# Prompt attention's units at other steps of a page-streaming attention, with first queries and row constants rounded in other steps

## The reference, cut to what matters

```python
logit[t, s] = q_t . k_s / sqrt(Dh) + cq[t] - ck[s]       # 16 heads of 64; c: running sum of log forget
s = where(k_pos <= q_pos, s, -1e30)
p = softmax(s, axis=-1)
o = einsum('bhqk,bkhd->bqhd', p, v)
```

## Time and profile before

| | us |
|---|---|
| median of three runs | 1809.26 |
| lowest, highest | 1804.97, 1809.34 |
| profiled execution | 1808.28 |
| its span, first to last instruction | 1806.5 |
| TensorE busy, share of the span | 1741.4, 96% |
| VectorE, ScalarE, GpSimd busy | 1151.8, 885.1, 348.6 |
| the attention stage | about 972 to 1347 |

### The profile page before, as it was taken

How to read it: one execution, slowest core, us unless ns; L and a number is a source line. 1 busy time by engine, 2 the same in 40 slices (tenths; PEclk the granted TensorE clock), 3 DMA queues, 4 the chain that set the end, 5 groups by cost and what they waited for, 6 DMA issues and landing times. The chain is left out here.

```text
span 1806.5 us, 41781 instructions
## 1 busy us (share of the span) xinstructions
PE 1741.4 (96%) x16593; PEld 1616.2 (89%) x16593; DVE 1151.8 (64%) x2113; ACT 885.1 (49%) x1579; POOL 348.6 (19%) x261
## 2 busy tenths in 40 slices
PE   8999999999999999999998999999989999999998
PEld 7999998889999999999997677776769999999998
DVE  4766775579828828555653466666656994595481
ACT  5355445465525524455632455555555653354252
POOL 3333332000120130333531011112200004003012
PEclk9999999899999999999999999999999999999999
DMA  5333222323423332342356999999983334234232
GB/s 129 85 108 85 83 84 66 87 79 94 118 71 94 95 94 71 87 147 62 117 172 205 384 374 379 385 385 367 366 287 99 94 94 117 61 97 115 57 100 70
DMA packets 291541, 273.79 MB, mean 152 GB/s; under 512 B 22034, under 2 KB 252531, under 8 KB 290836
## 3 DMA queue, kind: packets, MB, share of 16 engines
q1 hardware_dynamic: 289412, 268.63, 45.8%
q10 hardware_dynamic: 1792, 1.44, 0.3%
q0 software_dynamic: 144, 1.05, 0.2%
HBM read 254.64 MB, written 16.43 MB: 150 GB/s over the span
## 5 line engine op out<-in xcount | busy, mean ns | idle before, releaser
L2117 PE MATMUL ps<-xh,f_l 128*128 128x288 f32 x1232 | 279.2, 298 | 0.2 <-DVE f_l L2373 0.2
L2137 PE MATMUL ps<-f_h,f_l 128*128 128x288 f32 x1748 | 243.0, 296 | 0.2 <-DVE t_small L2482 0.2
L2137 PEld LDWEIGHTS ps<-f_h,f_l 128*128 128x128 f32 x1748 | 236.1, 189 | 0.4 <-DVE t_small L2482 0.4
L2117 PEld LDWEIGHTS ps<-xh,f_l 128*128 128x128 f32 x1232 | 208.6, 189 | 0.6 <-DVE f_l L2373 0.5
L2117 PE MATMUL ps<-xl,f_l 128*128 128x288 f32 x704 | 208.3, 296 | 0.0
L2117 PE MATMUL ps<-f_l 128*128 128x288 f32 x1056 | 156.8, 297 | 7.6 <-ACT t_small L2264 4.2
L2447 DVE TENSOR_TENSOR xT<-xT,ps 128x576 f32<-128x576 f32 x48 | 36.2, 754 | 197.1 <-PE ps L2137 197.1
L1586 DVE COPY at_kt<-ps 128x512 f32<-128x512 f32 x128 | 88.2, 691 | 109.7 <-PE ps L1289 109.2
L2117 PEld LDWEIGHTS ps<-f_l 128*128 128x128 f32 x1056 | 146.2, 189 | 9.0 <-ACT t_small L2264 5.0
L2117 PEld LDWEIGHTS ps<-xl,f_l 128*128 128x128 f32 x704 | 133.6, 190 | 0.0
L653 POOL TENSOR_TENSOR a_wl<-a_wraw,a_wh 128x1024 fp32r<-128x1024 f32 x32 | 78.5, 2456 | 200.6 <-ACT a_wh L548 185.4
(11 more groups left out here) (434 smaller groups left out, 4064.4 us busy)
## 6 DMA issues: line engine op xcount, KB each, us to landing
xT<-in_cache_k SPq DMA_DIRECT2D x40, 512.0 KB, 6.1
xT<-in_cache_v SPq DMA_DIRECT2D x40, 512.0 KB, 6.6
a_wraw<-in_a_w_in SPq DMA_DIRECT2D x32, 512.0 KB, 4.2
f_h_plain<-in_cache_k SPq DMA_DIRECT2D x30, 512.0 KB, 6.4
xl_plain<-in_cache_v SPq DMA_DIRECT2D x30, 512.0 KB, 6.5
f_h_plain<-in_cache_v SPq DMA_DIRECT2D x30, 512.0 KB, 7.0
xl_plain<-in_cache_k SPq DMA_DIRECT2D x29, 512.0 KB, 6.3
a_wraw<-in_w_gate_up SPq DMA_DIRECT2D x44, 256.0 KB, 4.1
```

What stands on the lines that cost most here:

```text
L2117: mm = pe.matmul(place(m, pos), wt[:, at], combination(2 * q, part, b), start=pos in (0, 1, 3) and t == 0 and i == 0, stop=t == len(pairs) ...
L2137: mm = pe.matmul(ps[:, first + a, 0:HALF], wt[:, at], hidden(i, part)[:, a * HALF:(a + 1) * HALF], start=opens and t == 0 and y == 0, stop ...
```

## The change

The head pairs' first steps are spread evenly from step 9 to step 64: 9, 16, 24, 32, 40, 48, 56, 64 in place of 15, 22, 29, 36, 43, 50, 57, 64. Within a head pair nothing changes: four steps, and the turns one step later. `unit_rows` and the casts of later queries move with the starts. The first head pair's query casts (`query_high(0)`) move from step 9 to step 4, and the rounding of the row constants from step 2 to step 4, where it stands before those casts.

```diff
-    FIRST_UNIT, PAIR_STEPS, PARTS_AT, OUT_AT, TAIL_AT = 15, 7, 4, 5, 6
+    PARTS_AT, OUT_AT, TAIL_AT = 4, 5, 6
+    FIRST_UNIT, LAST_UNIT = 9, KSTEPS
+    STARTS = [FIRST_UNIT + j * (LAST_UNIT - FIRST_UNIT) // (KD - 1) for j in range(KD)]
...
+    def unit_at(n):
+
+        j = sum(start <= n for start in STARTS) - 1
+        return j, n - STARTS[max(j, 0)]
+
     def unit_pair(n):
 
-        j, i = divmod(n - FIRST_UNIT, PAIR_STEPS)
-        return 4 * j + i if 0 <= j < KD and i < 4 else None
+        j, i = unit_at(n)
+        return 4 * j + i if j >= 0 and i < 4 else None
...
-                j = (n - AHEAD - 3 - FIRST_UNIT) // PAIR_STEPS + 1
-                if (n - AHEAD - 3 - FIRST_UNIT) % PAIR_STEPS == 0 and 1 <= j < KD:
-                    unit_rows(j)
+                if n - AHEAD - 3 in STARTS[:-1]:
+                    unit_rows(STARTS.index(n - AHEAD - 3) + 1)
...
-                if n == 2:
+                if n == 4:
                     act.wait_ge(e["headed"], 16)
                     act.activation(rowl[:], headrow, ACT.Copy).then_inc(e["fixed"], 1)
...
-                j, i = divmod(n - FIRST_UNIT, PAIR_STEPS)
-                if i == OUT_AT and 0 <= j < KD:
+                j, i = unit_at(n)
+                if i == OUT_AT and j >= 0:
                     output(j)
-                if n == FIRST_UNIT - 6:
+                if n == 4:
                     query_high(0)
                 if i == PARTS_AT and 0 <= j < KD - 1:
                     query_high(j + 1)
```

## The result

The changed kernel takes 1812.44 us in the median of 18 runs (1808.81 to 1816.20), the kernel before 1808.57 us (18 runs, 1802.99 to 1811.02): a ratio of 1.0025, 95% interval 1.0017 to 1.0034, so 3.1 to 6.1 us slower.

A forecast was written before the change was run, and what follows sets the result against it. TensorE was taken as the bound. Terms of 7.7 (units), -3.4, -1.7, +0.9 and +0.5 summed to +4.0 us on 1808.28, so 1812.3, stated as 1812.5; 8 in 10 range 1802 to 1819.

The forecast's parts named there:

- TensorE bound, parts add: Attention steps: TensorE is the bound, a step costs its parts' prices, and each microsecond it waits lengthens the span.
- Six groups at 8c: Head pairs starting at 16, 24 to 56, with a sequence's first exponential: 2.45 us of stalls each, 14.7 in all.
- First group: Head pair at steps 9 to 13: stalls like those of steps 57 to 61, 1.8 us.
- Part 2: Row constants rounded at step 4 instead of 2: ScalarE's wait for their transfer goes, gaining 3.4 us.
- Part 3: First queries cast at step 4 instead of 9: 1.7 us gained at step 10, 0.9 lost at step 5.
- The +0.9 for step 5: First query casts at step 4 make step 5's key copies late: 0.9 us lost (0 to 1.3).
- step 10 near its parts plus 0.8: Sign: step 10 would take about 0.8 us above its parts, though with a unit in it.
- Part 4: End of the stage, after light steps 61 to 63: last steps could wait for a page, +0.5 us (0 to 2).
- The sum: Whole kernel: all terms together +4.0 us, 1812.3 on the profiled execution, stated as 1812.5.
- The rival of the smoothed load: Units at a fixed place stall 3.5 us in place of 8.8: 1798.8 us; chance 0.15 for faster by over 0.3%.

The follow-up runs named there:

- E8: Changed kernel with the last key tile's four transposes done twice in the light steps from 21 on: 1821.58 us, ratio 1.0072 to the kernel before.
- E1: Kernel before with only the row constants rounded at step 4 instead of 2: 1805.97 us, ratio 0.9989.
- E5: Changed kernel with head pairs starting at 9, 17, 25, 33, 41, 49, 57, 64: 1811.14 us, ratio 1.0016 to the kernel before.
- E6: Changed kernel with head pairs starting at 10, 18, 26, 34, 42, 50, 57, 64: 1799.98 us, ratio 0.9959 to the kernel before.
- E7: Changed kernel with the sequence's exponential before the two unit exponentials in ScalarE's order within a step: 1804.13 us, ratio 0.9978 to the kernel before.
- E2: Kernel before with only the first queries cast at step 4 instead of 9: 1806.72 us, ratio 0.9993.
- E4: Changed kernel with the row constants back at step 2 and the first queries cast at step 3: 1814.75 us, ratio 1.0038 to the kernel before.
- E10: Kernel before with row constants and first query casts at step 4, and ScalarE's sequence exponential before the unit exponentials: 1801.33 us, ratio 0.9963.

## Why the prediction was right, step by step

- **TensorE bound, parts add.** Right, and shown by E8. Between kernels steps of the same make-up mostly agree within 0.03 us (a few within 0.1: step 31 took 5.87 us before and 5.78 in E1).
- **Six groups at 8c, 2.45 us each, 14.7.** Measured 2.32 (0.77, 0.80, 0.23, 0.52), 13.9. I had 1.0, 0.75, 0.1 and 0.6. E5 and E6 show that it is the phase, E7 that half of it is the place of one exponential in ScalarE's list: 1.14 of 2.32. The other half was not taken apart by a run of its own.
- **First group, 1.8.** Too small: 1.75 at step 10 (8.32 - 4.09 - 1.16 - 1.32) and 0.95 at step 13, with step 11 about as predicted: 2.8. I took step 58 as its model. But step 9, with no value mix for TensorE, is 4.11 us long where step 57 was 5.03 (it began at 1278.76, and step 58 at 1283.79), and ScalarE's chain in it is as long; so the copies of step 10 are later. Step 10 began at 1007.15 and its first key copy comes 2.60 us into it, step 58's came 1.47. With the exponential first, 1.40 of the 1.75 are gone. ScalarE's key copies of step 10 (changed) and of step 58 (before):

```profile
1009.75 1.07 ACT L1455 ACTIVATE at_kt<-ps 128x512 f32<-128x512 f32 x2
```

```profile
1285.26 1.07 ACT L1449 ACTIVATE at_kt<-ps 128x512 f32<-128x512 f32 x2
```

- **Part 2, -3.4.** Right in the profiled pair (3.43); 2.3 in the median of E1. The wait for the transfer is not the same in each execution, which can make this difference.
- **Part 3, -1.7 and +0.9.** The gain exists alone (E2: 1.56), yet step 10 of the changed kernel still lost 1.75: the unit put at step 9 brought the same lateness back that the casts had caused. The two terms stand in my sum apart, and that sum comes out right; but I did not see that they are one queue. The +0.9 for step 5 measured 0.3. One of the signs named beforehand, step 10 near its parts plus 0.8, did not come: 1.75.
- **Part 4, +0.5.** The size met the profiled pair (0.6), the place was wrong: there was no wait for a page. TensorE's busy time after step 62 was the same (25.79 us), but ScalarE waited 3.6 instead of 1.9 us for the next stage's weights. Nor does the size repeat: from step 63 to the first matmul of the next stage the other kernels with these starts took 32.54 (E4), 32.42 (E7) and 32.85 us (E8), and all kernels with other starts 32.41 to 32.43, against 33.01 and 32.41 in the pair.
- **The sum.** Measured terms: 13.9 + 2.8 - 8.8 - 3.4 - 1.7 + 0.3 = 3.1, less 0.4 because step 9 took 4.11 us with and without a unit: 2.7, against 2.5 in the windows. With 0.6 at the end 3.1, against 4.0 predicted and 3.9 between the medians. So the errors partly cancelled: the first group cost 1.0 us more than I had, while the six groups cost 0.8 less, step 5 0.6 less and step 9 0.4 less. That 1812.5 meets the median to 0.1 us is luck. The 0.8 us between profile and medians lie within what part 2's varying wait can make (1.4 to 3.4 us); that this is their cause was not tested.

Why ScalarE's wait for the next stage's weights grew is open. It was 3.6, 3.1, 2.9 and 2.4 us in the four kernels with a head pair at step 56 (changed, E4, E7, E8) and 1.2 to 2.5 in the others, one execution each; that the weights queue behind later pages was not tested.

The rival of the smoothed load (1798.8) was 13.6 us too low. The Trainium skill (Perfetto Trace Analysis, Optimization Strategy) holds that interleaving regimes with different bounds may help; E6 and the changed kernel show both sides: interleaved nearly evenly, the same work came out 8.7 us below the kernel before or 3.9 above it, by where it met the sequence's exponentials.

## What to carry to other kernels

When a hand-ordered stream with a fixed period carries a second load, choose the second load's phase before its spacing: price each step from single-step windows, and keep the loads from meeting on the engine that copies for the bound one. Where one engine's list puts long work behind work whose input comes later, try the long work first; here its input came 0.6 us earlier, and moving one loop was worth 8.3 us in the medians. A gain proved alone can be undone by what is put into the freed step.

## What was not expected

Step times repeat closely: the six groups of the changed kernel gave 6.62 or 6.63 us for 8c+1. Against that, one small transfer (the row constants) kept ScalarE waiting 4.35, 3.33 and 3.5 us in three executions (before, E2, E4), and the granted clock fell behind it in the first and the last. At the start of the stage the first step took 4.57 instead of 3.51 us in E7 and in E10, at a mean granted clock of 0.63.
